# Second residual chain of a two-layer block: order of the weight loads around the expert gathers, and the norm's scaling done by TensorE

## The reference, cut to what matters

```
x = x + mod[5] * (w0 * y0 + w1 * y1)          # y0, y1: the token's two expert outputs
h = x * rsqrt(mean(x*x) + eps) * g * (1 + scale) + shift
u = h @ w_in                                   # the mLSTM's input projection, 1024 -> 4096
```

## Time and profile before

| | |
|---|---|
| median of the runs | 2457.94 us |
| the profiled execution | 2461.31 us |
| its span | 2459.7 us |
| TensorE busy | 2321.2 us (94%) |
| VectorE busy | 1625.6 us (66%) |
| ScalarE busy | 946.8 us (38%) |
| moved by DMA | 649.12 MB, mean 264 GB/s |

### The profile page before, as it was taken

How to read it: one execution, slowest core, us unless ns; L and a number is a source line. 1 busy time by engine, 2 the same in 40 slices (tenths; PEclk the granted TensorE clock), 3 DMA queues, 4 the chain that set the end, 5 groups by cost and what they waited for, 6 DMA issues and landing times.

```text
span 2459.7 us, 42712 instructions
## 1 busy us (share of the span) xinstructions
PE 2321.2 (94%) x16387; PEld 1553.2 (63%) x16388; DVE 1625.6 (66%) x2005; ACT 946.8 (38%) x1167; POOL 427.6 (17%) x461
## 2 busy tenths in 40 slices
PE   6999989999999999999969999999999899999984
PEld 3555534457888888888847887666644455555542
DVE  2899985447898889888976651677534633454544
ACT  3000014115777777777754232466421111111111
POOL 0633431220000000000020000211000223233323
PEclk8999989999999999999989999999999899999997
DMA  9111075539999999999992132212543979999997
GB/s 342 58 44 59 34 293 167 182 113 402 421 401 388 380 395 383 385 389 392 378 380 81 62 124 104 87 54 75 193 154 140 412 313 376 404 421 420 420 420 309
DMA packets 154320, 649.12 MB, mean 264 GB/s; under 512 B 27866, under 2 KB 42874, under 8 KB 99458
## 3 DMA queue, kind: packets, MB, share of 16 engines
q1 hardware_dynamic: 126624, 577.40, 59.7%
q0 software_dynamic: 16192, 57.53, 6.5%
q10 hardware_dynamic: 11426, 13.12, 1.5%
HBM read 595.13 MB, written 52.86 MB: 263 GB/s over the span
## 4 chain that ended last, share of the span: by engine, by line
PE 81%; DMA 9%; DVE 4%; ACT 2%; issue 2%; POOL 1%; SPq 0%; ACTq 0%; DVEq 0%; POOLq 0%
PE ps L970 78%; DMA arena<-in_w_dram 6%; DMA chunk<-in_w_ada_dram 1%; ACT arena L1616 1%; DVE arena L2380 1%; PE ps L1212 1%; PE ps L1190 1%; PE ps L1196 1%; DMA arena<-h_d,uix 1%; PE ps L1059 1%; POOL arena L769 0%; DMA buf_d<-arena 0%; PE ps L1586 0%; DMA arena<-in_w_ada_dram 0%; DMA arena<-buf_d,slots 0%
## 5 line engine op out<-in xcount | busy, mean ns | idle before, releaser
L970 PE MATMUL ps<-arena 128*32 128x256 f32 (+5 forms) x10296 | 1188.7, 407 | 38.9 <-DVE arena L2380 12.3
L970 PEld LDWEIGHTS ps<-arena 128*32 128x32 f32 (+1 forms) x10296 | 652.5, 129 | 521.1 <-issue 318.5
L2433 DVE TENSOR_TENSOR wl<-wx,wh 128x2048 fp32r<-128x2048 f32 x228 | 511.1, 2285 | 18.5 <-ACT wh L1616 18.5
L1616 ACT ACTIVATE arena<-ps 128x256 f32<-128x256 f32 (+5 forms) x389 | 176.4, 478 | 864.0 <-PE ps L970 616.9
L1616 ACT ACTIVATE wh<-wx 128x2048 fp32r<-128x2048 f32 x228 | 432.4, 1915 | 80.8 <-PE ps L970 75.9
L2380 DVE COPY arena<-arena 128x2048 f32<-128x2048 f32 x180 | 222.7, 1297 | 273.1 <-PE ps L970 228.8
L970 PE MATMUL ps<-wh,xT 128*128 128x512 f32 x1184 | 379.2, 394 | 1.2 <-issue 0.7
L970 PEld LDWEIGHTS ps<-wh,xT 128*128 128x128 f32 x1184 | 222.5, 188 | 53.1 <-issue 1.2
L2502 DVE SCALAR_TENSOR_TENSOR arena<-arena,par 128x768 f32<-128x768 f32 x232 | 241.1, 1112 | 0.0
L970 PE MATMUL ps<-wl,xT 128*128 128x512 f32 x608 | 239.4, 394 | 0.0
L970 PE MATMUL ps<-wh,gT 128*128 128x512 f32 x608 | 199.5, 399 | 0.0
(11 more groups left out here) (362 smaller groups left out, 2267.1 us busy)
## 6 DMA issues: line engine op xcount, KB each, us to landing
wx<-in_w_dram SPq DMA_DIRECT2D x228, 1024.0 KB, 8.4
arena<-in_w_dram SPq DMA_DIRECT2D x192, 1024.0 KB, 21.8
arena<-in_w_ada_dram SPq DMA_DIRECT2D x40, 1024.0 KB, 8.6
craw<-in_w_in_c_dram SPq DMA_DIRECT2D x8, 2048.0 KB, 8.7
buf_d<-arena POOLq DMA_DIRECT2D x1, 14848.0 KB, 57.5
arena<-buf_d POOLq DMA_DIRECT2D x19, 512.0 KB, 10.0
buf_d<-arena POOLq DMA_DIRECT2D x19, 512.0 KB, 7.7
arena<-in_w_in_ab_dram SPq DMA_DIRECT2D x8, 1024.0 KB, 12.6
```

Source lines behind the costliest of these rows:

```text
L970: return pe.matmul(bank_ap, lhsT, rhs, start=first, stop=last)
L1616: return act.activation(out_, in_, f, **kw)
L2433: v.tensor_tensor(wl[:, g], wx[:, g], whs[g % NH].bitcast(F32), ALU.subtract).then_inc(m["low"], 1)
```

## The change

- ScalarE no longer scales the tile. VectorE multiplies the identity by the column of reciprocals (a 128x128 diagonal, two buffers `turn`), and TensorE, in place of transposing the scaled tile against the identity, multiplies the raw tile by that diagonal, which turns and scales it at once. `norm` writes its squares to one scratch tile, and VectorE waits before it overwrites a diagonal until the products that read it are done.
- GpSimd's useless load of 512 KB becomes one row of 4 KB. GpSimd waits for the last store itself and starts the gathers `y0` without ScalarE's `done`.
- SyncE: items 16 to 19 as before; then a wait until the third gather `y0` (index 2) has landed; then `craw`; then items 20 to 23. Items 24 to 27 are issued after the last tile's new x and its store, again not before `mods(20)`.
- TensorE: `mods(20)` to `mods(23)` move behind tile 3's turn, the turn of vectors 4 and 5 behind the last tile, and `mods(24)` to `mods(27)` behind that, ahead of the projection. Vector 6 is made in bank 7 in place of bank 0; the projection's pass ct = 3 waits for its eviction.
- ScalarE: `vector_out(5)` moves behind the loop over the tiles, `vector_out(6)` and the wait for the stores of x behind the modulation. VectorE takes `low_slice(0)` ahead of its wait for the turned vectors.

```diff
-                    if n == 2 and i == 0:
-                        sp.wait_ge(x_new, j + 1 - NT)
+                    if n == 2 and i == len(tiles) - 1:
                         sp.wait_ge(u_mm, 21)
                         for k in range(24, 28):
                             item_load(k)
-                    if n == 2 and i == 2:
-                        sp.dma_start(craw, wc[:, :, 0:512]).then_inc(cw, 16)
...
-            for n in range(16, 24):
+            for n in range(16, 20):
                 sp.wait_ge(moe["used"], nb * PAIRS + (n - 16 + 4))
                 item_load(n)
+            sp.wait_ge(y_in[2], y_gathered(2, 2))
+            sp.dma_start(craw, wc[:, :, 0:512]).then_inc(cw, 16)
+            for n in range(20, 24):
+                item_load(n)
...
-                pool.dma_start(xg, buf_v[:, bass.ds(nb + 1, 1), :].rearrange("p a d -> p (a d)")).then_inc(m["xg"], 16)
+                pool.dma_start(xg[0:1, :], buf_v[0:1, bass.ds(nb + 1, 1), :].rearrange("p a d -> p (a d)")).then_inc(m["xg"], 16)
...
+                pool.wait_ge(m["yst"], nb * 16 + 16)
+                pool.sem_inc(pool_s, 1)
...
-                if n == 2:
-                    pool.wait_ge(moe["done"], 1)
-                else:
+                if n == 4:
                     pool.wait_ge(un["copied"], NX * PAIRS)
...
-                src = hall[:, t, :] if n in (1, 3) else CH[n]["h"][j % 2]
+                src = hall[:, t, :] if n in (1, 3) else CH[n]["xt"][x_place(n, j)]
...
+                    if n in (1, 3):
+                        ins = pe.transpose(to, pairs(src)[:, k // 2, k % 2, :], ident)
+                    else:
+                        ins = mm(to, src[:, k * P:(k + 1) * P], CH[n]["turn"][j % 2], True, True)
...
-            for n in range(16, 24):
+            for n in range(16, 20):
                 mods(n)
             for t, j in tiles_of(2):
                 to_channels(2, t, j)
-                if t == 4:
-                    for n in range(24, 28):
+                if t == 3:
+                    for n in range(20, 24):
                         mods(n)
-                if t == 2:
+                if t == NT - 1:
                     pe.wait_ge(u_ev, 6)
...
+            for n in range(24, 28):
+                mods(n)
...
+                if ct == 3:
+                    pe.wait_ge(u_ev, 7)
...
-                    if n == 2:
-                        scaled(n, t, j)
                     if n == 2 and t:
                         turned(n, t - 1, j - 1)
-                    if n == 2 and t == 0:
-                        vector_out(5)
                 if n == 2:
+                    vector_out(5)
                     act.wait_ge(cw, 16)
                     go(cw0h, craw[:, :, 0:P], ACT.Copy).then_inc(c_high, 1)
-                    vector_out(6)
                     turned(n, t, j)
...
+                        if j - 2 >= tl[0][1]:
+                            v.wait_ge(tr_rdy, j - 1)
+                        v.wait_ge(rs_rdy, t + 1)
+                        v.tensor_scalar(ch["turn"][s], ident, rs[:, s:s + 1], None, ALU.mult).then_inc(h_rdy, 1)
...
-VBANK = (0, 1, 2, 3, 0, 2, 0, 6, 0, 2)
+VBANK = (0, 1, 2, 3, 0, 2, 7, 6, 0, 2)
```

More of the change, by code:

```diff
@@ L289, in chain_arrays @@
                         tmp=at(43120, D), htt=at(44144, KD, P),
-                        h=[at(12288 + D * i, D) for i in range(2)],
+                        h=[at(12288, D)], turn=[at(13312 + P * i, P) for i in range(2)],
                         y=[[at(o + D * i, D) for i in range(NT)] for o in (44144, 6144)])
@@ L1057, in to_channels @@
                 for k in range(KD):
-                    part = pairs(src)[:, k // 2, k % 2, :] if n in (1, 3) else src[:, k * P:(k + 1) * P]
-                    ins = pe.transpose(ps[:, 4 + k // 4, (k % 4) * P:(k % 4 + 1) * P], part, ident)
+                    to = ps[:, 4 + k // 4, (k % 4) * P:(k % 4 + 1) * P]
+                    if n in (1, 3):
+                        ins = pe.transpose(to, pairs(src)[:, k // 2, k % 2, :], ident)
+                    else:
+                        ins = mm(to, src[:, k * P:(k + 1) * P], CH[n]["turn"][j % 2], True, True)
                 ins.then_inc(tr_rdy, 1)
@@ L1639, in norm @@
                 s = j % 2
-                dst = hall[:, t, :] if n in (1, 3) else CH[n]["h"][j % 4 if n == 4 else s] if n else sqs[s]
+                dst = hall[:, t, :] if n in (1, 3) else CH[n]["h"][j % 4 if n == 4 else 0] if n else sqs[s]
                 src = CH[n]["xt"][x_place(n, j)] if n else x0[:, t, :]
@@ L1645, in norm @@
                     act.wait_ge(x_new, j + 1 - NT)
-                if n == 2 and j - 2 >= tiles_of(n)[0][1]:
-                    act.wait_ge(tr_rdy, j - 1)
                 if j >= 2:
@@ L1663, in turned @@
                 go(dst, psf[:, 4 * 512:6 * 512].rearrange("p (k n) -> p k n", n=P), ACT.Copy).then_inc(ht_rdy, 1)
-            def scaled(n, t, j):
-                act.wait_ge(rs_rdy, t + 1)
-                go(CH[n]["h"][j % 2], CH[n]["xt"][x_place(n, j)], ACT.Copy, scale=rs[:, j % 2:j % 2 + 1]).then_inc(h_rdy, 1)
             def chain(n):
@@ L1849, in experts @@
                 go(ss[:, 0:1], ones[:, 0:1], ACT.Copy).then_inc(m["done"], 1)
+                act.wait_ge(m["done"], 1)
             for i in range(3):
@@ L1948, in _ @@
             act.wait_ge(h_rdy, 3 * NT)
-            await_stores(act, 3)
             act.wait_ge(a_mm, 3)
@@ L1963, in _ @@
                 n += 1
+            await_stores(act, 3)
             for ct in range(1, 4):
                 high_slice(ct)
+            vector_out(6)
             vector_store(6)
@@ L2531, in low_chunk @@
                 low(KE + KD * g + k, (slice(None), k, slice(None)))
+            low_slice(0)
             v.wait_ge(a_mm, 3)
@@ L2539, in _ @@
             v.tensor_copy(mB[:].rearrange("p (c h) v -> p c h v", h=2), turned[:, 0, :, :, 0:2]).then_inc(md_v, 1)
-            low_slice(0)
             v.wait_ge(md_v, 8)
```

## The result

The change made the kernel slower: 2468.73 us, median of 18 runs (2463.93 to 2472.05), against 2459.55 us of the kernel before beside it (18 runs, 2457.22 to 2465.3). The ratio is 1.0034 [1.0028, 1.0041], 9 us. I had forecast 2460.5 us and a range up to 2466. The profiled execution took 2465.81 us (span 2464.0).

A forecast was written before the change was run, and what follows sets the result against it. The prediction saw two limits at the seam, a chain's latency and bytes to move. The first pass's end moving from 1313.3 to 1315.9 gave +2.6 us, so 2460.5 us against the median 2457.94; range 2451 to 2466.

The forecast's parts named there:

- (a): GpSimd's y1 gathers: without the 512 KB load ahead, all six land one queue slot, 2.65 us, earlier.
- (b): Store and y0 gathers: with emptier DMA, store 4.7 us, gather 5.3, GpSimd's wait saves 0.4; 4 us won.
- (c): Loads behind the third gather: 13.8 MB at 404 GB/s take 34.1 us, so item 27 lands at 1301.9.
- (d): Scaling in the tiles' turn: eight products take 1.9 us, 3.9 at half clock; covered by waiting for item 23.
- (e): TensorE's order: mods(20) to mods(23) take 5.6 us, hTx complete at 1298.5 to 1302, no better than before.
- (f): mods(24) to mods(27) ahead of the projection wait for item 27, take 5.6 us; first pass 8.4, ending 1315.9.
- A: Rival, faster: bytes are no limit, items 20 to 27 arrive when wanted; -10 us, 2448 us; chance 0.18 whole or part.
- B: Rival, slower: store and gathers stay slow, third gather lands after 1269; +6.4 us, 2464.3 us; chance 0.16.
- C: Rival, slower: eight products cost four times the transposes, 7.8 us at clock 0.50; +23 us, 2481 us; chance 0.04.

The follow-up runs named there:

- the third of the kernel after: The changed kernel, unchanged, timed and profiled a third time: 2469.76 us, ratio 1.0034 to the kernel before.
- the seven profiles: Three of the changed kernel, four variants: ScalarE scaling again, GpSimd's part undone, its wait undone, unused TensorE products added; experts' end to first pass's end 66.0 to 69.5 us.
- the kernel without the fold: The changed kernel with ScalarE scaling each tile again and TensorE transposing it, no diagonal; loads and order stay: 2468.56 us, ratio 1.0036.
- the kernels with early loads: Changed kernel with items 20 to 23 right behind 16 to 19, items 24 to 27 right behind craw: 2459.13 us; with GpSimd's part also undone 2455.94 us.
- TensorE kept busy: Ten unused 128x512 products (the filling) added to the changed kernel with early item loads and GpSimd's part undone: 2454.67 us, ratio 0.9977.

## Why the prediction was wrong

**What held.** The mechanism is the one forecast, and its signs of proof came: an emptier DMA at 1252 to 1267, a full stretch to 1303, TensorE idle behind the last turn for a load of `w_ada`. The end of the first pass is set by item 27.

**(a) half failed.** The last y1 gather is issued 13.5 us ahead of the experts' end in both kernels (1238.71, 1239.60 after), so the load's place in the queue moved no issue; the first y1 add came 1.2 us earlier against that end, not 2.65 (1251.33 at an experts' end of 1253.12; 1251.62 at 1252.23). It cost nothing, as the tiles wait for item 23 later.

**(b) right in sum, wrong in both terms.** The store took 2.98 us, not 4.7; GpSimd's wait took 1.14 us, not less than before's 0.5. The third gather landed at 1267.02, with the experts' end 0.9 us later than before; I had 1266.7. On the store, the Trainium skill ("DMA: Bandwidth & Descriptors", anatomy of a GpSimd DMA; 3.2 us by estimate) was nearer than the nearest rows: 2.98 us lies within 0.3 us of it.

**(c) is the step that failed: the time of 13.8 MB behind the third gather.** I took 35.2 us from the third gather's landing to item 27 (1.1 until data flows and 34.1 at 404 GB/s). The first profile shows 38.5 (1267.02 to 1305.52), the third of the kernel after 40.3, the mean of the seven profiles 39.3. The bytes were right (13.7 MB by the windows from 1268 to 1308); three things were left out of the rate, the first partly in my 1.1 us, an estimate that no row gave. The start: 306 GB/s from 1268 to 1272, 1.0 us. The dip at the hand-over from the x stores to items 24 to 27: 0.8 us in the first profile ((404 - 365) x 8 / 404), 1.9 in the third. The end: bulk data stop near 1303, and the last item counts as landed 2.5 us later.

I had written that issue is no limit, because the stores would still fill the engines until 1291.5; in the third profile they did, nearly to the microsecond, and that left no room for item 23 being late. I had it 19.7 us behind the third gather (1286.4 - 1266.7); it came 21.1 to 23.9 us behind it in the seven profiles, 22.3 on average. The DMA view from the third gather's landing to item 23's tells why (queue: packets, MB, share), in the first profile of the kernel after (1267.02 to 1288.24) and in the third (1267.56 to 1291.00):
```profile
q1 hardware_dynamic: 2259, 6.80, 84.5%
```
```profile
q1 hardware_dynamic: 2469, 7.57, 83.2%
```
This is SyncE's queue. In these windows it has issued `craw`, items 20 to 23 and the stores of x. `craw` and items 20 to 23 are 6.29 MB; the other 0.5 and 1.3 MB are stores of x, which stand behind item 23 in the queue and were moved before it was complete. I had counted only what stands ahead of it. With the gathers' bytes (1.33 and 1.37 MB, not 1.2) this makes 1.6 and 3.6 us at 404 GB/s, against 1.5 and 3.7 measured; it fits the seven profiles within 0.2 us. From item 23's landing to item 27's it takes 16.4 to 17.4 us in all seven, 17.0 on average where I had 15.5, so the scatter of item 27 is mostly that of item 23. Of the 4.1 us by which (c) came out too short, 2.6 lie ahead of item 23's landing and 1.5 behind it. My lower bound of the rate, 377 GB/s, came from full stretches and held neither the hole nor the end.

**(d), (e), (f) held.** Eight products take 3.75 to 3.79 us at clock 0.50 and 2.02 at 1.00 (forecast 3.9 and 1.9), covered by item 23, as the kernel without the fold shows. hTx was complete at 1298.6 (1298.5 to 1302). Vector 6 took 5.3 us and the first pass 8.6 (5.6, 8.4).

**The sum.** Forecast +2.6 us; the stretch says +5.0 in the first profile and +6.4 on average over the seven. The time says +8 to 9. Of the 8.2 us between forecast and result, 3.8 are the stretch, where step (c) stands, and 1.6 the median of three runs from which I started (2457.94; 2459.55 over 18). Some 2 to 3 us stay open: two of the three profiles of the kernel after lie 2.9 and 3.8 us below the medians of its runs and the third on it, and stages that the change does not touch scatter by as much.

**Rivals.** A (bytes no limit) did not come for this kernel; the kernels with early loads show that a gain needs another order of loads: 5.7 us from the first gather on, the fold with it. B needed the third gather after 1269; it landed at 1266.7 to 1267.6 in the three profiles of the kernel after (1265.0 to 1268.5 over the seven), and the loss of B's size came from another place. C is refuted: products against transposes at the same clock are 3.77 to 1.94 us and 2.02 to 1.09, a factor of 1.9; the factor of four that the Trainium skill states ("TensorE: Matmul & The Clock Gate", Terms) is not seen in these runs. My range failed because it treated (c) as a rate between two steady rates.

**A better version.** With items 20 to 23 loaded as before, items 24 to 27 right behind craw, the fold kept, GpSimd's part undone and TensorE kept busy: 2454.67 us, 0.9977 [0.9968, 0.9985] of before, some 14 us below the kernel after. The chain of the same kernel without the filling:
```profile
1251.76 7.34 DMA buf_d<-arena
...
1259.60 6.44 DMA arena<-buf_d,slots
...
1271.62 2.07 PE ps L968 x16
...
1304.36 120.69 PE ps L968 x689
```
Store and gather are slow again, 13.8 us together, and still this kernel is ahead: the bytes are moved in that time, and no load of weights is left in the chain.

## What to carry to other kernels

In this kernel, latency won by emptying the DMA engines was paid back with the bytes that had not moved meanwhile; hold loads back only if something else has slack for all of them. The time of the last of a row of loads is bytes over the full rate plus its start, its end (2.5 us here) and any hole where a load waits for work that waits for an earlier load. A load in the middle of the row was late by bytes that stand behind it in the queue (0.5 to 1.4 MB here), so leave what waits for it that room. Before forecasting to 0.2%, look at what one profiled execution scatters by: here up to 4.6 us outside the stretch in question, between two profiles of one kernel. Where a part of the kernel repeats, measure there: from the first gather to the end of the first pass the fold's 3.4 us stand out of a scatter of less than 0.1 among kernels with the same loads.

## What was not expected of the hardware

- GpSimd waiting for its own store needs 1.13 to 1.14 us until the next gather; with a copy of ScalarE in between (0.21 us) it is 0.5.
- In the first profile of the kernel after, the last of a row of loads is reported 2.5 us after the bulk of its data: DMA share 0.87 at 1302 to 1303, then 0.21 and 0.07.
- SyncE's queue moved 0.5 to 1.4 MB of transfers issued later before item 23, issued earlier, was complete.
- Eight transposes every 3.72 us leave the granted clock at 0.50, eight products every 3.23 us hold it at 1.00; both take some 2 us, so the form with twice the work costs no time.
